# SSM mixing head prepared inside the SSM projection, with a staggered order of the last two weight units and paired post norms

## The reference, cut to what matters

```
cum = jnp.cumsum(dtc * a, axis=2)
seg = cum_t[..., :, None] - cum_t[..., None, :]
lmat = jnp.where(lower_tri, jnp.exp(jnp.where(lower_tri, seg, 0.0)), 0.0)
cb = jnp.einsum('bcigs,bcjgs->bcgij', cc, bc)
y = jnp.einsum('bcgij,bcghij,bcjghp->bcighp', cb, lmat, xdt)
...
y = y + xc * d_skip[..., None]
...
xc_new = xc + mods_c[2] * rms_norm(y[:, :L], n_post)
return xc_new, x + mods_x[2] * rms_norm(y, n_post)
```

## Time and profile before

| | |
|---|---|
| median of 3 runs | 2847.22 us |
| profiled execution, its own time | 2845.64 us |
| its span, first to last instruction | 2844.3 us |
| PE busy | 2616.6 us, 92% |
| DVE, ACT, POOL busy | 1457.9, 1299.1, 762.5 us |
| mixing stage of layer 0 | 139.7 to 281.0 us, PE busy 130.2 |
| mixing stage of layer 1 | 1433.6 to 1531.0 us, PE busy 80.7 |

### The profile page before, as it was taken

How to read it: one execution, slowest core, us unless ns; L and a number is a source line. 1 busy time by engine, 2 the same in 40 slices (tenths; PEclk the granted TensorE clock), 3 DMA queues, 4 the chain that set the end, 5 groups by cost and what they waited for, 6 DMA issues and landing times. The chain is left out here.

```text
span 2844.3 us, 34994 instructions
## 1 busy us (share of the span) xinstructions
PE 2616.6 (92%) x13281; PEld 2128.3 (75%) x13281; DVE 1457.9 (51%) x1709; ACT 1299.1 (46%) x1677; POOL 762.5 (27%) x346
## 2 busy tenths in 40 slices
PE   6998999999998799998988898887799999999997
PEld 4775778877777688877765787666688888888885
DVE  2476321433522422202465325443788888888886
ACT  2571423321442322223553334253577677777765
POOL 0330443234223244433323545534100000000000
PEclk9999999999999899999989999998799999999998
DMA  7275232123112233322264433412799999999997
GB/s 228 74 234 181 89 89 75 60 89 87 47 54 95 70 93 90 102 78 87 75 211 159 120 96 110 119 60 74 271 363 342 333 372 355 332 353 359 351 327 280
DMA packets 234571, 496.55 MB, mean 175 GB/s; under 512 B 14864, under 2 KB 111408, under 8 KB 234288
## 3 DMA queue, kind: packets, MB, share of 16 engines
q1 hardware_dynamic: 232544, 494.20, 51.1%
q10 hardware_dynamic: 1872, 0.26, 0.1%
HBM read 493.37 MB, written 1.05 MB: 174 GB/s over the span
## 5 line engine op out<-in xcount | busy, mean ns | idle before, releaser
L290 POOL TENSOR_TENSOR unit_lo<-raw_units,unit_hi 128x1024 fp32r<-128x1024 f32 x244 | 589.4, 2438 | 1087.0 <-ACT unit_hi L282 1087.0
L2639 DVE TENSOR_TENSOR moe_unit_lo<-moe_raw,moe_unit_hi 128x2048 fp32r<-128x2048 f32 (+1 forms) x283 | 612.0, 2175 | 103.5 <-ACT moe_unit_hi L2633 100.5
L2633 ACT ACTIVATE moe_unit_hi<-moe_raw 128x2048 fp32r<-128x2048 f32 (+1 forms) x280 | 509.1, 1821 | 218.9 <-PE bank L311 216.8
L282 ACT ACTIVATE unit_hi<-raw_units 128x1024 fp32r<-128x1024 f32 x246 | 246.6, 1052 | 508.3 <-PE bank L311 419.1
L309 PE MATMUL bank<-unit_hi,hT_hi 128*128 128x256 f32 (+1 forms) x1168 | 420.3, 360 | 32.1 <-PEq L1341 13.7
L310 PE MATMUL bank<-unit_lo,hT_hi 128*128 128x256 f32 (+1 forms) x1168 | 399.0, 342 | 0.0
L311 PE MATMUL bank<-unit_hi,hT_lo 128*128 128x256 f32 (+1 forms) x1168 | 398.6, 341 | 0.0
L309 PE MATMUL bank<-moe_unit_hi,xe_T_hi 128*128 128x512 f32 (+1 forms) x768 | 290.4, 378 | 1.1 <-DVE xe_T_lo L2670 1.1
L310 PE MATMUL bank<-moe_unit_lo,xe_T_hi 128*128 128x512 f32 (+1 forms) x768 | 287.0, 374 | 0.0
L311 PE MATMUL bank<-moe_unit_hi,xe_T_lo 128*128 128x512 f32 (+1 forms) x768 | 286.2, 373 | 0.0
L309 PEld LDWEIGHTS bank<-unit_hi,hT_hi 128*128 128x128 f32 x1168 | 225.6, 193 | 79.1 <-issue 42.7
(11 more groups left out here) (401 smaller groups left out, 4175.9 us busy)
## 6 DMA issues: line engine op xcount, KB each, us to landing
moe_raw<-in_moe_w SPq DMA_DIRECT2D x224, 1024.0 KB, 7.4
raw_units<-in_w_in SPq DMA_DIRECT2D x160, 512.0 KB, 3.7
moe_raw<-in_moe_w SPq DMA_DIRECT2D x64, 768.0 KB, 4.3
ada_unit<-in_ada_w SPq DMA_DIRECT2D x40, 1024.0 KB, 5.2
raw_units<-in_ffn_w SPq DMA_DIRECT2D x66, 512.0 KB, 3.8
raw_units<-in_w_branch SPq DMA_DIRECT2D x48, 512.0 KB, 3.6
ada_first<-in_ada_w SPq DMA_DIRECT2D x8, 1024.0 KB, 13.7
raw_units<-in_w_out SPq DMA_DIRECT2D x16, 512.0 KB, 3.5
```

The source lines that it names most:

```text
L282: act.activation(half_of(view(whi, g), half), half_of(view(raw, g), half), ACT.Copy).then_inc(hi_ready, 1)
L290: eng.tensor_tensor(lo, whole, hi.bitcast(F32), ALU.subtract).then_inc(lo_ready, 1)
L2633: act.activation(moe_hi[:, at_unit % RING, 0:n], moe_raw[:, at_unit % SLOTS, 0:n], ACT.Copy).then_inc(hi_m, 1)
L2639: dve.tensor_tensor(moe_lo[:, at_unit % SLOTS, 0:n], moe_raw[:, at_unit % SLOTS, 0:n], moe_hi[:, at_unit % RING, 0:n].bitcast(F32), ALU.su ...
```

## The change

The sums of decay rates, their splitting on DVE, `dt_delta` and `ssm_skip` go from the head of `ssm_mix` into `ssm_project` (PE: third block of columns, after its second quarter; DVE: behind the convolution of the second block). In `ssm_mix` the first decay matmul no longer waits for `skip_coef`, which is now made behind the first `mix`; ACT's part of the filler in slot 6 comes behind the first side products, and the head has less filler. The last two weight units of both output stages are used in another order of tiles. `PostNorm` handles tiles in pairs, and the next stage's first split lies in front of the last pair.

```diff
+        def last_two(n):
+            if n == 2:
+                return [(0, 0), (0, 1), (1, 0), (1, 1)]
+            return [(0, 0), (0, 1), (0, 2), (1, 0), (1, 1), (0, 3), (1, 2), (1, 3)]
...
 ssm_project, vector:
                     ins.then_inc(dt_dve, 1)
+                    dve.wait_ge(dt_dve, 3)
+                    for tile in q_tiles:
+                        for d in range(2):
...
+                            ins = dve.tensor_copy(dta_rows[:, c:c + 64]...
+                    ins.then_inc(rows_ready, 1)
+                    dve.tensor_tensor(skip[:, :], hp[:, 72:88], hp[:, 88:104], ALU.add)
+                    dve.tensor_tensor(delta[:, :], dtv[:, 0:64], dtv[:, 64:128], ALU.subtract)
                     dve.wait_ge(cum_sum, 1)
...
                     conv(1)
+                    dve.wait_ge(cum_turned, 1)
+                    sel = const("row_sel")
+                    c, a, b = ps[7][:, lo_tok:TOK], cum_part[:, lo_tok:TOK], cum_hi[:, lo_tok:TOK]
+                    dve_step(dve, dve.tensor_copy(b, c))
+                    dve_step(dve, dve.scalar_tensor_tensor(a, b.bitcast(F32), sel[:, 0:1], c, ALU.mult, ALU.add))
+                    dve.tensor_scalar(cum_lhs[:, lo_tok:TOK], ...)
+                    dve.tensor_scalar(cum_row[:, lo_tok:TOK], ...)
                     dve.wait_ge(exps_done, 1)
 ssm_project, tensor:
+                                if n == 2 and u == 0 and k == 1:
+                                    cum_turns()
...
-        Z_TAIL, Z_HEAD = [0, 0], [6, 6]
+        Z_TAIL, Z_HEAD = [0, 0], [3, 3]
...
 ssm_mix, scalar:
-                    fill.act(act, 6)
                     for m in range(slots):
...
-                            if m == 0:
+                            if m == 3:
                                 act.wait_ge(coef_ready, 1)
...
                             ins.then_inc(side_done, 1)
+                            if m == 0:
+                                fill.act(act, 6)
 ssm_mix, vector:
+                    spread_rows(tiles[0])
                     for i in range(len(jobs) // 4):
                         dve.wait_ge(cb_sum, i + 1)
+                        dve.tensor_copy(cbs[i][:, :, :], ...).then_inc(cb_out, 1)
+                    dve.wait_ge(cb_out, len(jobs) // 4)
                     segments(0)
+                    spread_rows(tiles[1])
...
                         mix(m)
+                        if m == 0:
+                            skip_weights()
 ssm_mix, tensor:
-                    fill.pe(pe, 6)
-                    pe.wait_ge(lhs_ready, 1)
-                    pe.wait_ge(coef_ready, 1)
                     for m in range(halves + 3):
...
                             last.then_inc(seg_sum, 1)
+                        if m == 0:
+                            fill.pe(pe, 6)
+                            pe.wait_ge(cb_out, len(jobs) // 4)
                         modulation(m)
...
 PostNorm:
+            def act(self, act, between):
+                for j in range(0, self.n, 2):
+                    if j == self.n - 2:
+                        between()
+                    for b in self.banks_of():
+                        self.square(act, j, b)
+                    self.root(act, j)
+                    for b in self.banks_of():
+                        self.square(act, j + 1, b)
+                    self.x_square(act, j)
+                    self.root(act, j + 1)
+                    self.x_root(act, j)
+                    self.x_square(act, j + 1)
+                    self.x_root(act, j + 1)
+            def dve(self, dve):
+                for j in range(0, self.n, 2):
+                    self.mean(dve, j)
+                    self.add(dve, j)
+                    self.mean(dve, j + 1)
+                    self.x_mean(dve, j)
+                    self.add(dve, j + 1)
+                    self.out(dve, j)
+                    self.x_mean(dve, j + 1)
+                    self.out(dve, j + 1)
...
 out_project and ffn_down, scalar:
-                    split_hi(act, b0)
-                    post.act(act)
+                    post.act(act, lambda: split_hi(act, b0))
 ffn_down, tensor (out_project alike, with one bank a tile and four k):
+                    for u, tile in last_two(NT):
+                        pe.wait_ge(lo_ready, 2 * (b0 - 2 + u + 1))
+                        for b in range(2):
+                            for k in range(2):
+                                last = down(b0 - 2 + u, k, tile, b)
+                            if u and tile == NT - 1 and b == 0:
+                                last.then_inc(tile_done, 1)
+                        if tile == NT - 1:
+                            last.then_inc(unit_used, 1)
+                        elif u:
+                            last.then_inc(tile_done, 1)
```

More of the change, by code:

```diff
@@ L979, in ssm_mix @@
             inters = [x for x in steps if x[0] > 0 and ORDER[x[1]][x[0]] in tiles]
-            lo_tok = tiles[0] * P
             halves = 2 * len(jobs)
@@ L1162, in modulation @@
                             ada_rows(pe, ps[4][:, 0:256], ada_buf[i % 2], u, u == 0, u == ADA_U - 1).then_inc(ada_used, 1)
-                    pe.wait_ge(rows_ready, 1)
-                    for tile in tiles:
-                        for d, tri in enumerate(("tri_f", "tri_b")):
-                            last = pe.matmul(ps[0][64 * d:64 * d + 64, tile * P:(tile + 1) * P],
-                                             dta_rows[:, tile * P + 64 * d:tile * P + 64 * d + 64], const(tri), start=True, stop=True)
-                    last.then_inc(cum_turned, 1)
                     for n, (tile, g) in enumerate(jobs):
@@ new lines, in banks_of, with root, x_square @@
+            def banks_of(self):
+                return (1,) if self.early else (0, 1)
+            def root(self, act, j):
+                r = post_sq[:, 2 * j:2 * j + 1]
+                act.wait_ge(self.means, j + 1)
+                act.activation(r, r, ACT.Sqrt).then_inc(self.roots, 1)
+            def x_square(self, act, j):
+                tile = self.tiles[j]
+                act.wait_ge(self.x_out, j + 1)
+                if j:
+                    act.wait_ge(self.x_squared, j)
+                act.activation(self.x_junk[:, :], xres[:, tile, :], ACT.Square,
+                               accum_out=x_sq[:, tile:tile + 1]).then_inc(self.x_squared, 1)
@@ new lines, in x_root @@
+            def x_root(self, act, j):
+                r = x_sq[:, self.tiles[j]:self.tiles[j] + 1]
+                act.wait_ge(self.x_means, j + 1)
+                act.activation(r, r, ACT.Sqrt).then_inc(self.x_roots, 1)
+            def act(self, act, between):
[12 more added lines that the diff above has]
+                    self.x_root(act, j + 1)
@@ new lines, in mean, with add @@
+            def mean(self, dve, j):
+                for b in self.banks_of():
+                    self.weigh(dve, j, b)
+                a, c = (post_sq[:, 2 * j + i:2 * j + i + 1] for i in range(2))
+                dve_step(dve, dve.tensor_scalar(a, a, c, 1.0 / D, ALU.add, ALU.mult))
+                dve.tensor_scalar(a, a, EPS, None, ALU.add).then_inc(self.means, 1)
+            def add(self, dve, j):
+                tile, r = self.tiles[j], post_sq[:, 2 * j:2 * j + 1]
+                dve.wait_ge(self.roots, j + 1)
+                dve_step(dve, dve.reciprocal(r, r))
+                dve.wait_ge(self.weighed, self.index[j, 1] + 1)
+                x = by_group(xres[:, tile, :])
+                dve.scalar_tensor_tensor(x, self.y[:, :, of_tile(tile)], r, x, ALU.mult, ALU.add).then_inc(self.x_out, 1)
@@ new lines, in x_mean, with out @@
+            def x_mean(self, dve, j):
+                r = x_sq[:, self.tiles[j]:self.tiles[j] + 1]
+                dve.wait_ge(self.x_squared, j + 1)
+                dve.tensor_scalar(r, r, 1.0 / D, EPS, ALU.mult, ALU.add).then_inc(self.x_means, 1)
+            def out(self, dve, j):
+                tile = self.tiles[j]
+                dve.wait_ge(self.x_roots, j + 1)
+                dve_step(dve, dve.reciprocal(x_sq[:, tile:tile + 1], x_sq[:, tile:tile + 1]))
+                self.after(dve, tile)
```

167 lines of the change are left out of this document (67 added, 100 removed).

## The result

The changed kernel took 2866.03 us (median of 4 runs, 2864.95 to 2868.12); the kernel before, timed beside it, took 2848.47 (4 runs, 2845.05 to 2851.84). The ratio is 1.0062 with a 95% interval of 1.005 to 1.0075: slower by 17.6 us. The forecast was 2858 and slower, +11; the sign is right, the time lies at the upper edge of the range, just outside it.

The account below looks back on a forecast made before the run. PE, busy 92% of the span, was taken as the bound. Layer 0 +8.2, layer 1 +3.1 and tails -0.2 gave +11.1 us on 2845.64, so 2856.7; with 1.6 for the median 2858, range 2849 to 2866.

Parts of the forecast that it names:

- Part 1: Projection: the cumulative sums add PE matmuls there, +1.0 us in layer 0 and +0.6 in layer 1.
- Part 2: Mixing heads: ACT's later split delays the first modulation unit and PE waits, +3.7 us in layer 0, +3.3 in layer 1.
- The first rival: Mixing heads: the modulation unit is not waited for, so the kernel gets faster, 2832 us; chance 0.07.
- Part 3: Mixing heads: filler weight six to three moves steps to where PE is full, +2.6 us in layer 0, +0.7 in layer 1.
- Part 4: Mixing stages: half clock after PE's idle time, +0.9 us in layer 0; layer 1's cold stretch shrinks, -1.5.
- Part 5: Output tails: layer 0's projection +1.1 us and down projection +0.9, additions stretched beside POOL; layer 1's projection -2.2.
- The third rival: Mixing stages: after the idle both layers work long at half clock, about +20 us, 2867; chance 0.12.

Follow-up runs that it names:

- e5: The changed kernel with the filler's head weight back at six instead of three in both layers; 2850.51 us, ratio 0.9999.
- e3: The changed kernel with SP issuing the first two modulation units before the reload of the filler's raw buffer; 2844.45 us, ratio 0.9989.
- e6: The changed kernel with both modulation units issued ahead of the filler's first unit and head weight six; 2833.64 us, ratio 0.9941.
- e11: The kernel before with the filler's head weight three instead of six, nothing else; 2862.49 us, ratio 1.0041.
- e4: The changed kernel with ACT splitting the filler's second unit at the stage's entry, as before the change; 2856.29 us, ratio 1.0024.
- e10: The changed kernel with head weight six in layer 0 and three in layer 1; 2862.98 us, ratio 1.0039.
- e9: e5 with the head giving up as many filler steps as the changed kernel, run right behind the head, later steps unmoved; 2850.80 us, ratio 0.9997.
- e2: The kernel before with only the change's tails: new order of the last two units and paired post norms; 2845.14 us, ratio 0.9993.
- e8: The kernel before with the two modulation units issued ahead of the filler's first unit, nothing else; 2847.44 us, ratio 0.9989.

## Why the forecast was half right

The medians by the two causes, as ratios to before: changed kernel 1.0062; filler's place mended (e5) 0.9999; unit's issue mended (e3) 0.9989; both (e6) 0.9941. Each costs 14 to 21 us where the other is present or not; what the change gains, with both mended, is 17 us. The parts don't simply add. e5 is the change with all but its third part; the forecast for that is 11.1 - 3.3 = +7.8, and e5 measured nothing (-2.9 to +2.0 us). Beside the weight of 3 the same parts cost about +6 (1.0062 against e11's 1.0041).

- **Part 1, the sums**: forecast +1.0 and +0.6. From the turn of `normed` to the barrier -0.4 in layer 0, +0.4 in layer 1. Slightly too large; no experiment isolates it.
- **Part 2, the late unit**: right in place and in time. First use 19.9 and 17.3 us after the barrier forecast, 19.8 and 17.8 measured; idle of 10 and 12 forecast, 9.6 and 11.0 measured. e3 and e4 show the cause. What the lateness costs in the end, +3.7 and +3.3 in the forecast, is not confirmed: e5 has it and took no longer than before. The first rival (the unit is not waited for) was put at 2832. The run in which that is so with all else as changed is e3, and it took 2844.5, since the rival too priced the weight at +3.3. That e6 took 2833.6 is a coincidence, for it has the other weight. What decided against the rival was SyncE's queue, as the prediction had it.
- **Part 3, the filler's weight**: this is the step that failed. The prediction counted the steps that leave the head, 2 and 1 of 1.44 us, and priced their own work at +2.6 and +0.7 with 4.3 as the upper bound. The one number also moves every later step, and that was never asked. It costs 11.3 us by itself (e11) and 15.5 to 18 in the changed kernel (e5), most of it in layer 1 (e10). By the profiles about 4 of that is own work, near the bound, and the rest is longer waits and half clock behind the head. How much each contributes no run separates: e9 left the steps ahead of the unit. With 11.3 in the place of 3.3 the sum would have been +19.1 against +17.6 measured, but e5 shows that the other terms were too large where the weight is 6, so part of this closeness is luck.
- **Part 4, the clock**: layer 1's -1.5 fits e9 (108.9 us behind the first unit, before 110.2), but two kernels with before's weight and sums, e2 and e8, ran 109.1 and 113.1, so it is not confirmed. For the changed kernel the sign is wrong: 24.8 us at half clock where before had 16.1. Layer 0's +0.9 can't be judged from one profile: e2 and e8 (the latter with two issues swapped) needed 165.5 and 165.6 us from the C-B matmuls to the turn of `y_ssm`, the profile of before 161.1, with 20.5 us at half clock against 10.2 behind the first unit. e5 needed 167.5, the changed kernel 172.9. The short profile of before is also why its +9 in layer 0 seemed to match the sum.
- **Part 5, the tails**: right. +1.1 and -2.2 forecast in the output projections, +0.9 and -2.3 measured; +0.9 forecast in the down projection, +0.8 measured (PE's idle time there 10.49 and 11.25). The addition was stretched by POOL's piece as forecast: it was to start at 943.2 and end at 946.0, 1.5 us later than by itself, and it took 2.83 us instead of 1.28. (The prediction's 2.3 us is the effect on both tails together.)
- **The third rival**, a long cold stretch at 2867, had the right number for another reason. The half-clock stretch around the unit's arrival is 10.2 us in layer 0 and 13.7 in layer 1 in the trace, but PE worked for 3.5 and 4.4 us of these. Much of the cost lay in waits and short stretches far behind the head.

## What to carry to other kernels

When a table of weights changes one entry, list where each later step lands, and not only how many the entry gives up: here the steps given up were at most 4.3 of 11 to 18 us. When an experiment moves work out of a slot, count on the trace what stands ahead of the wait in question, for the next slot may still be in front of it. Look for pieces of GpSimd that fall on short two-input operations of VectorE that TensorE waits for, and read the longest wait of a line beside its total. Before work is put ahead of a buffer's release, follow what stands behind that release in the DMA queue: here one issue moved by a line was worth 21 us.

## What was not expected of the hardware

- Two mixing stages with the same total wait for one operation (6.2 and 6.3 us) had 24.8 and 11.7 us at half clock. In the changed kernel full clock was lost behind PE's waits of 2.2 and 2.7 us for it; behind the pieces of 0.6 to 1.7 us in e9 it was not. Length alone does not decide: a wait of 1.4 us for `segments`, 7 us behind the first unit, was followed by a stretch in both kernels, and in e3, which has the same waits for `x_weighted` (6.2 us, the longest 2.7), PE went on at full clock behind the one of 2.21 us that ended at 1490.92:

```profile
1490.90:1500.00 9.10, 8.68 (x67) 1.00 0.62 193
```

  What does decide stays open.
- GpSimd's piece stretched a VectorE operation of 0.68 us up to 2.77 and one of 1.28 to 2.83.
- Nearly the same head in different kernels (before, e2, e8) gave 161.1 to 165.6 us for the same stage, almost all of it by half-clock stretches that fell differently (PE idle 9.6 to 9.8 us behind the first unit in all three). A single profile does not settle 4 us here; the medians do.
